# Differential attention scores: 64-partition contractions, two maps in turn into two buffers

## What is computed

```python
def probs(qb, kk):
    s = jnp.einsum("bqhd,bkhd->bhqk", qb, kk).astype(jnp.float32) * scale
    return jax.nn.softmax(s, axis=-1)

def one(qbs):
    p = probs(qbs[0], k)
    if q2 is not None:
        p = p - lam * probs(qbs[1], k2)
    return jnp.einsum("bhqk,bkhe->bqhe", p.astype(v.dtype), v)
```

## Time and profile before

| | |
|---|---|
| time, median of 3 | 2922.69 us (2919.51 to 2923.07) |
| span of the profiled execution | 2919.1 us |
| TensorE busy | 2739.9 us, 94% |
| VectorE busy | 1317.6 us, 45% |
| ScalarE busy | 696.5 us, 24% |
| differential attention, layer 0 | 665.90 to 742.16 us |
| differential attention, layer 1 | 2103.14 to 2179.40 us |

### The profile page before, as it was taken

One profiled execution on the slowest core, in us unless ns is written; L12 is line 12 of the kernel. 1 busy time (PEld: TensorE's weight loads), 2 busy tenths in 40 slices (PEclk: granted clock), 3 DMA queues, 4 the chain that ended last, 5 costly groups with the idle time before them and its releaser, 6 DMA issues.

```text
span 2919.1 us, 46013 instructions
## 1 busy us (share of the span) xinstructions
PE 2739.9 (94%) x17468; PEld 2439.4 (84%) x17468; DVE 1317.6 (45%) x1748; ACT 696.5 (24%) x1190; POOL 1289.1 (44%) x580
## 2 busy tenths in 40 slices
PE   5999998998999899999989999999899998999996
PEld 3954897786999799999958469968779998999996
DVE  4324326697223644253233342467772256353352
ACT  2122333505321211011022223253153112010011
POOL 1501452150565466666534025513405654666663
PEclk8999999999999999999979999999999999999998
DMA  6222121020122322222242411201102223222221
GB/s 252 80 92 79 53 75 37 16 71 17 59 73 69 109 76 72 72 79 72 76 164 71 138 40 60 74 16 37 65 9 73 73 70 109 75 72 73 78 72 50
DMA packets 61647, 215.13 MB, mean 74 GB/s; under 512 B 6832, under 2 KB 10160, under 8 KB 61232
## 3 DMA queue, kind: packets, MB, share of 16 engines
q1 hardware_dynamic: 56448, 203.97, 20.8%
q10 hardware_dynamic: 5040, 8.99, 0.9%
HBM read 208.44 MB, written 4.49 MB: 73 GB/s over the span
## 4 chain that ended last, share of the span: by engine, by line
PE 78%; DVE 10%; ACT 3%; DVEq 3%; issue 3%; DMA 2%; ACTq 1%; POOL 0%; POOLq 0%; SPq 0%
PE big L399 19%; PE big L403 19%; PE big L402 19%; PE big L532 4%; PE last_two L563 2%; PE two L546 2%; DVE sq L1491 2%; PE big L635 1%; PE last_two L659 1%; DMA raw<-in_w 1%; PE big L422 1%; PE big L660 1%; PE big L425 1%; PE big L426 1%; PE two L480 1%
## 5 line engine op out<-in xcount | busy, mean ns | idle before, releaser
L358 POOL TENSOR_TENSOR w_hi<-raw,cst 128x1024 fp32r<-128x1024 f32 x288 | 555.4, 1928 | 1549.5 <-PE big L399 1189.1
L399 PE MATMUL big<-act_hi,w_hi 128*128 128x320 f32 x2784 | 878.5, 316 | 27.2 <-DVE act_lo L1560 9.6
L402 PE MATMUL big<-act_lo,w_hi 128*128 128x320 f32 x2784 | 869.4, 312 | 0.0
L403 PE MATMUL big<-act_hi,w_lo 128*128 128x320 f32 x2784 | 869.2, 312 | 0.0
L361 POOL TENSOR_TENSOR w_lo<-raw,w_hi 128x1024 fp32r<-128x1024 f32 x288 | 733.6, 2547 | 44.1 <-issue 8.0
L399 PEld LDWEIGHTS big<-act_hi,w_hi 128*128 128x128 f32 x2784 | 530.4, 191 | 35.7 <-issue 16.7
L402 PEld LDWEIGHTS big<-act_lo,w_hi 128*128 128x128 f32 x2784 | 530.8, 191 | 1.5 <-issue 0.4
L403 PEld LDWEIGHTS big<-act_hi,w_lo 128*128 128x128 f32 x2784 | 530.0, 190 | 0.0
L399 PE MATMUL big<-ff_hi,w_hi 128*128 128x320 f32 x1024 | 316.9, 309 | 4.1 <-DVE ff_lo L1150 4.1
L402 PE MATMUL big<-ff_lo,w_hi 128*128 128x320 f32 x1024 | 315.3, 308 | 0.0
L403 PE MATMUL big<-ff_hi,w_lo 128*128 128x320 f32 x1024 | 315.2, 308 | 0.0
(11 more groups left out here) (293 smaller groups left out, 3676.3 us busy)
## 6 DMA issues: line engine op xcount, KB each, us to landing
raw<-in_w SPq DMA_DIRECT2D x384, 512.0 KB, 3.3
x<-in_x ACTq DMA_DIRECT2D x1, 2560.0 KB, 10.8
out_y<-x SPq DMA_DIRECT2D x8, 320.0 KB, 2.4
cst<-in_const ACTq DMA_DIRECT2D x1, 1938.5 KB, 16.3
small<-in_small ACTq DMA_DIRECT2D x2, 505.0 KB, 4.5
out_C<-c_new ACTq DMA_DIRECT2D x2, 256.0 KB
v_d<-in_past ACTq DMA_DIRECT2D x2, 256.0 KB, 2.8
k_d<-in_past ACTq DMA_DIRECT2D x2, 256.0 KB, 3.0
```

What stands on the lines that cost most here:

```text
L358: nc.gpsimd.tensor_tensor(w_hi[:, to, :], raw[:, slot, :], ones[:, 0:1].to_broadcast([P, BLK]), ALU.mult)
L399: first = mm(ps, wh, ah, start=k == 0, stop=False)
L402: mm(ps, wh, al, start=False, stop=False)
L403: last = mm(ps, wl, ah, start=False, stop=k == nk - 1)
```

## The change

The scores read the queries from `q_d` directly, 64 partitions for each map, against the same 64 partitions of `k_d`. The zero-padded copies, their memsets and their semaphore are gone. `scores` first waits for both buffers and then issues half 0 of map 0, half 0 of map 1, half 1 of map 0, half 1 of map 1. For the latent attention, which has one map, the order stays as it was.

```diff
-        q_map = [stage, sq]
...
-                    if maps == 2 and t == 0:
-                        pe.wait_ge(q_map_ready, l * H_D + h + 1)
+                    use = FIRST_USE[name] + maps * i
+                    n = (k1 - k0) // (1 if t == LATE else 2)
                     for m in range(maps):
-                        use = FIRST_USE[name] + maps * i + m
-                        wait_free(pe, l, use)
-                        ps, b, _ = buf(use)
-                        n = (k1 - k0) // (1 if t == LATE else 2)
-                        for c in range((k1 - k0) // n):
+                        wait_free(pe, l, use + m)
+                    for c in range((k1 - k0) // n):
+                        for m in range(maps):
+                            ps, b, _ = buf(use + m)
                             last = mm(ps[:, c, 0:n], q_of(h, m)[:, q0:q1], k_of(h, m)[:, k0 + c * n:k0 + c * n + n],
                                       start=True, stop=True)
-                        last.then_inc(ready[b], 1)
+                            if c == (k1 - k0) // n - 1:
+                                last.then_inc(ready[b], 1)
...
-                attend(l, "da", 2, 1, 40, 4, lambda h, m: q_map[h % 2][:, m, :], lambda h, m: k_d[:, h, :],
+                attend(l, "da", 2, 1, 40, 4, lambda h, m: q_d[64 * m:64 * m + 64, h, :], lambda h, m: k_d[64 * m:64 * m + 64, h, :],
...
-                        h, t = units[i + 1]
-                        if maps == 2 and t == LATE and h + 2 < heads:
-                            lay_out(h + 2)
...
-                for tile in q_map:
-                    for m in range(2):
-                        other = 64 * (1 - m)
-                        v.memset(tile[other:other + 64, m, :], 0.0)
-
-                def lay_out(h):
-
-                    for m in range(2):
-                        r = slice(64 * m, 64 * m + 64)
-                        v.tensor_copy(q_map[h % 2][r, m, :], q_d[r, h, :])
-                    dve.drain().then_inc(q_map_ready, 1)
-                lay_out(0)
-                lay_out(1)
```

More of the change, by code:

```diff
@@ L244, in trunk @@
         cond_done = sem("cond_done")
-        q_map_ready = sem("q_map_ready")
         gather_done, small_sum = sem("gather_done"), sem("small_sum")
@@ L1180, in merge, with attend @@
                         behind(m)
-            def attend(l, name, maps, side, unit0, set0, heads, prob, exp0, out, lay_out=None):
+            def attend(l, name, maps, side, unit0, set0, heads, prob, exp0, out):
                 units = attention_units(heads, side)
@@ L1495, in _ @@
                     dve.drain().then_inc(roped, 1)
-                for tile in q_map:
-                    for m in range(2):
-                        other = 64 * (1 - m)
-                        v.memset(tile[other:other + 64, m, :], 0.0)
-                def lay_out(h):
-                    for m in range(2):
-                        r = slice(64 * m, 64 * m + 64)
-                        v.tensor_copy(q_map[h % 2][r, m, :], q_d[r, h, :])
-                    dve.drain().then_inc(q_map_ready, 1)
-                lay_out(0)
-                lay_out(1)
-                attend(l, "da", 2, 1, 40, 4, H_D, prob_d, 40, q_d, lay_out)
+                attend(l, "da", 2, 1, 40, 4, H_D, prob_d, 40, q_d)
                 for h in range(H_D):
```

## The result

| | before | changed |
|---|---|---|
| time, median of 4 | 2921.1 us (2916.6 to 2923.1) | 2942.1 us (2940.7 to 2943.2) |
| span of the profiled execution | 2919.1 us | 2941.2 us |
| differential attention, layer 0 | 76.26 us | 85.50 us |
| differential attention, layer 1 | 76.26 us | 87.02 us |

The ratio is 1.0072 (95% interval 1.0060 to 1.0084): 21.0 us slower, where 15.4 us were forecast, inside the range of 2931 to 2953 us. The two stages account for 20.0 of the 22.1 us between the spans. The other 2 us are spread over the rest of the run, about 1 us of it ahead of the first stage.

What follows compares the result with a forecast made beforehand. The prediction took a loop between TensorE, VectorE and ScalarE to bound differential attention. Per layer, 6.1 us for the joined wait plus 1.6 for the clock, twice, made 15.4 us on 2922.69: 2938.1 us, range 2931 to 2953.

Steps and rivals of the forecast that it cites:

- What bounds the kernel: Differential attention, 76.3 us a layer: not plain TensorE; the loop between TensorE, VectorE and ScalarE can set the pace.
- VectorE's copies at zero: Removing roughly 8 us of VectorE memsets and copies in a layer gains zero, at most 2 us in a layer.
- The overlap: Scores on two row halves overlap: a full unit's 8 records take 5 slots, 1.35 us instead of 2.16, bringing nothing.
- The wait for both buffers: Scores' joined wait removes the maps' offset: loop 4.24 us against 3.18 to 3.82 before, +6.1 us in a layer.
- The clock: TensorE's clock falls once near each stage's start, to 1.2 of 2.4 GHz, for 1.5 loops: 1.6 us in a layer.
- rival 3: Clock stays low for five loops in each layer's differential attention: 2953 us; chance 0.08.
- Sum: Whole run: 2 x (6.1 + 1.6) = 15.4 us on 2922.69 gives 2938.1 us; chance 0.42.
- Without a fall of the clock: Differential attention: clock doesn't fall, everything else as forecast: 2934.9 us; chance 0.28.
- No overlap: Scores: the two halves don't overlap, map 0 ready after 6 slots, 0.54 us later in 32 full units: 2952 us; chance 0.14.
- Faster, by TensorE's time: Differential attention: TensorE's own work sets the pace, the wait for both buffers costs nothing: 2903.3 us; chance 0.03.

Runs made afterwards that it cites:

- e7: Changed kernel with VectorE's memsets and copies put back at their old places, read and waited for by nobody: 2940.4 us.
- e2: Kernel before, with scores waiting for both buffers before map 0's first product; padded copies and map order kept: 2935.3 us.
- e4: Changed kernel plus products nobody reads, filling TensorE's idle time ahead of the waits of units 1 to 3 of head 0 in each layer: 2935.5 us.
- e3: Kernel before on padded copies of 128 partitions, with the change's order: both waits first, then the two maps' halves in turn: 2955.8 us.
- e6: Changed kernel, same order of products, with the wait for map 1's buffer moved to just ahead of map 1's first half: 2929.2 us.
- e1: Changed kernel, still 64-partition scores, but map 0 issued whole and then map 1, each behind its own buffer's wait: 2927.6 us.
- e5: e1 plus products nobody reads, two ahead of unit 1's waits and one ahead of unit 2's in head 0 of each layer: 2921.8 us.

## Why the prediction was right, and where it was off

**What bounds the kernel** held. The stage was read as a loop between three engines, and 31 us less of score time on TensorE over the run bought nothing.

**VectorE's copies at zero** held to 0.3 us in a layer (e7).

**The overlap** held in its effect, and its picture was off. I took 5 slots, 1.35 us, with map 1 one record behind map 0. The records start in pairs, one of each map (the two at 689.01), so it is 4 slots, 1.08 us. The other 0.20 us of the 1.28 are at the two ends: 0.10 us more than a slot from the first pair to the second, and 0.10 us more from the last to the transposes. This second part is near the 0.12 us that I had set aside for going back to the whole array. Nothing hung on this: map 0 has its scores at the same time either way.

**The wait for both buffers** was the deciding term and held: 4.24 us worked out, 4.23 and 4.24 measured, 4.25 in e2. A head at full clock was put at 19.68 us. It is 19.70 us in e4's head 0, 19.91 and 19.75 us in heads 1 and 2 of the changed kernel's layer 0. In head 1's fourth unit the maxima start 0.16 us late, behind `normalise` and beside the copy into `q_d`. With the early falls of the clock filled (e4) the stages are 83.3 and 83.2 us where 82.4 was worked out, so this term was 0.8 to 0.9 us low in a layer. Up to 0.3 us of that comes in head 1, which has a later fall of the clock in e4. Another 0.4 us is in the last head and at full clock, in e4 as in the changed kernel. One distance there is 4.51 us and not 4.24:

```profile
737.14 1.35 PE L529 MATMUL big<-k_d,q_d 64*128 64x320 f32 x8 [1.51 <-ACT prob_d L863]
...
741.65 1.35 PE L529 MATMUL big<-k_d,q_d 64*128 64x320 f32 x8 [2.25 <-ACT rs L863]
```

ScalarE's two exponentials start 1.34 us apart in it (739.38 and 740.72), not 1.06. The kernel before has the same 1.34 us at this place (729.76 to 731.10). I took 1.06 from one pair for all of them. What ScalarE waits for there the trace does not name.

**The clock** was the step that was mis-sized. I expected one fall of 1.5 loops, 1.6 us in a layer. In layer 0 head 0 takes 689.01 - 666.88 = 22.13 us, 2.45 us over 19.68, and in layer 1 22.01 us. In layer 1 the clock fell again at the end of head 1 and of head 2, which take 21.11 and 20.18 us, and e4's stage there is 3.8 us shorter. Both layers together: 6.1 us by stages and 6.6 by medians, not 3.2. The sum allowed one fall near the start of a stage, but the loop leaves TensorE idle for over 1 us in every unit, all through the stage, and a fall can come later too. I had named this in rival 3 with a chance of 0.08. It came in part: two to four loops and not five.

**Sum.** Wait 2 x 7.0 us and clock 6.1 us make 20 us of stages, against 2 x 6.1 and 3.2 in the forecast. Both terms were low, so nothing cancelled; the growth is inside the range because the range was wide enough for it. The rest of the 22 us of span is outside the stages, where the traces differ by up to 5 us among themselves, and no step explains it.

**Rivals.** Without a fall of the clock (2934.9 us): close to e4's 2935.5, but in part by chance, since e4's stages are 1.7 us longer than this rival's and still have falls of the clock. No overlap (2952 us): e3 shows what it would have been, 2955.8. Faster, by TensorE's time: refuted by e2 and e6, in which only waits were moved.

## What to carry to other kernels

Two buffers in turn are worth the offset between their users. Before joining two waits at the head of a group, add up the loop: the last buffer's release, the first product, and then both users' work one behind the other. Here one wait moved ahead by two products (four records) cost 7 us in 76. The saving on TensorE didn't reach it, because it lay in map 1's scores, and TensorE waits behind those anyway. Time ahead of the end of map 0's scores would have counted, as e3 shows. And a faster step on TensorE inside a loop that others set makes idle time, and idle time can cost the clock: 64-partition scores with the right waits were slower than padded ones until the gap was filled.

## What the runs showed of the hardware

- Products of 64 partitions on the two row halves of the array ran side by side: 8 records of 320 columns in 1.28 us against 2.16 on the whole array, in turn or not (e1, 684.12). Where map 1's products were issued behind all of map 0's, its first still started 0.01 us behind map 0's first. The Trainium skill, TensorEngine Tiling (Array Packing), Theoretical Speedup, gives up to 2x where the contraction is 64 or less; with 1.7 the trace comes near.
- The clock fell from 1.00 to 0.50 at 669.3 us in the changed kernel, in the second of two waits (2.29 and 2.88 us) around 1.3 us of scores, and at 666.9 us in e1, at the end of the second of its two (2.20 and 1.70 us). In the kernel before, waits of 2.20 and 0.76 us around 2.3 us of scores left it at 1.00, and so did e5's filled ones. The length of one wait does not decide it: 2.29 us ahead of the first scores was enough in e2's layer 0 (low from 666.2 us), and in its layer 1 the same 2.29 us was not.
- At the lower clock the eight overlapping records take 2.50 us by the timeline, against 1.35 at the full one; the loop grows by 1.16 us.
